# Token tiles taken out of step at the stage changes of a two-block transformer kernel

## The chip, the cores and the metric

The kernel runs on one core of one Trainium2 chip. The metric is the device time of one execution in microseconds. Time before the change: 2136.25 us, the median of 3 runs (2133.06 to 2136.64).

## What is computed

256 tokens of width 1024 in fp32. The first block (a mixer of three attention kinds, then a mixture of experts gathered row by row) is untouched by the change except for its very end. The second block is:

```
for layer in (0, 1):
    x = x + 0.5 * norm(swiglu(norm(x)))        # ffn0, ffn2
    h = norm(x)
    m = short_conv(h)      if layer == 0       # conv_in, conv_out
      = diff_attention(h)  if layer == 1       # q, k, v -> o
    x = x + norm(m)
    x = x + 0.5 * norm(swiglu(norm(x)))        # ffn1, ffn3
    if layer == 0: k, v = norm(x) @ w_kv       # shared keys and values
```

Each norm is an RMS norm over the 1024 columns with its own gain. swiglu has 2816 hidden columns.

## The kernel before

**Tiling.** The tokens are two tiles (t = 0, 1) of 128. Every weight matrix is read in blocks ("panels") of 1 MB, 1024 x 256 or 256 x 1024 words. The list of panels is written once (`plan_panels`, lines 65 to 101), with the PSUM bank of each, and all engines follow it by semaphores that count panels. SyncE loads panel p into `raw[p % 3]` as soon as panel p - 3 is split (`load`, L411). Products are kept exact by splitting each fp32 operand into a high part (ScalarE copy to fp32r, L669) and a low part (VectorE subtraction, L1106), and by three matmuls per product (`exact3`, L1767: high x high, high x low, low x high, all recorded at L1759). ScalarE and VectorE split panel p once panel p - 3 is used.

**Two forms of a block.** `panel_a` keeps 128 weight columns stationary and moves 256 tokens (output: features on partitions). `panel_b` keeps 128 tokens stationary and moves 256 weight columns (output: tokens on partitions). Both are 48 matmuls of 256 columns.

**An ffn** (`ffn`, L2082) has 11 steps of a gate, an up and a down block. Gate goes to bank 0, up to bank 1; ScalarE takes silu (L960), VectorE the product (L1585), both split it into `ah`, `al` (L965, L1590). Down blocks add into four accumulator banks `ACC[2t + half]` over all steps: 24 matmuls of 512 columns, first tile 0 then tile 1. Steps 2 to 10 are a loop; the last down block stands alone.

**A stage change** (`post`: ScalarE L988, VectorE L1611, POOL L625). When tile t's sums are complete, ScalarE squares the 1024 columns (L995), POOL makes rstd (L529, L532), VectorE multiplies by the gain (L1619) and adds to x (L1622). Then the next norm: ScalarE squares and scales tile 0 (L1002, L1004), VectorE tile 1 (L1110, L1630). TensorE waits for both tiles and transposes 16 squares of 128 x 128 into `ACC` (`turn`, L1816); ScalarE and VectorE write them, 256 wide, times the gain of the next norm as `xh` (L708) and `xl` (L1127). The first block of the next stage starts on k = 0 as soon as its low part is there. ScalarE and VectorE split the next stage's first two panels before `post`.

**Around it.** conv_in is 12 blocks in the order b, c, u for each quarter; conv_out and o are `project` (L2112), four blocks of token-stationary matmuls straight into `ACC`, the last one's tile 0 announced by `branch_half`. After ffn1 the rows are normed for kv (8 blocks: 4 of k, 4 of v), and the same transposes, still in `ACC`, are written again with another gain for ffn2 (`turn("f2")`, L1037). q (4 blocks) comes after ffn2. In `turn("diff")` the normed attention output is transposed, and `project("o")` waits for all eight low parts (L2200).

```
2101  panel_a(p0, stream=f"f{f}")       # first gate block, waits for xl piece by piece
2102  panel_a(p0 + 1)
...
2137  for t in range(TT):
2138      pe.wait_ge(rows_ready[t], XIDX["f0"] + 1)
2139  turn("f0", xn)
```

Of the kernel before, what the change touches and what calls it, by code (L numbers as in the profile page):

```python
# [26 lines left out]
P = 128  # L27
# [37 lines left out]
def plan_panels():  # L65
# [3 lines left out]
    def add(name, count, pieces=1, words=PANEL, banks=(0, 1)):  # L69
        for j in range(count):  # L70
            b = banks[j % len(banks)] if banks else None
            plan.append((name, pieces, words, b))
# [20 lines left out]
    add("conv_in", 12, banks=(0, 1, 2))  # L93
    add("conv_out", 4, banks=())
    ffn("ffn1")
    add("kv", 8)
    ffn("ffn2")
    add("q", 4)
# [15 lines left out]
EVAC = [sum(b is not None for b in BANK[:p]) for p in range(NP + 1)]  # L114


XPOSE = [("mix", 4), ("hg", 2), ("peer", 4), ("f0", 4), ("conv", 4), ("f1", 4), ("kv", 4), ("attn", 4), ("diff", 4), ("f3", 4)]
XBASE = {n: sum(b for _, b in XPOSE[:k]) for k, (n, _) in enumerate(XPOSE)}
XEND = {n: XBASE[n] + b for n, b in XPOSE}
XIDX = {n: k for k, (n, _) in enumerate(XPOSE)}  # L120

_splits = [(n, 2 * b) for n, b in XPOSE]
_splits.insert(XIDX["kv"] + 1, ("f2", KD))
SBASE = {n: sum(b for _, b in _splits[:k]) for k, (n, _) in enumerate(_splits)}
SEND = {n: SBASE[n] + b for n, b in _splits}
# [18 lines left out]
SUMS = {n: sum(m not in HEAD_NORMS for m, *_ in NORMS[:k + 1]) for k, (n, *_) in enumerate(NORMS)}  # L144
# [3 lines left out]
X_AT = {n: 2 * (k + 1) for k, n in enumerate(["peer", "final", "p0", "pc", "p1", "p2", "pa", "p3"])}  # L148

POSTS = [("p0", "conv"), ("pc", "f1"), ("p1", "kv"), ("p2", "attn"), ("pa", "f3"), ("p3", None)]  # L150
# [10 lines left out]
def build(nc, io):  # L161
    ctx = ExitStack()
    with ctx:
# [6 lines left out]
        def over(name, shape, at, skip=0):  # L170

            return nc.alloc_sbuf_tensor_at(name, shape, F32, offset=place[at] + skip)
# [124 lines left out]
        top[0] = 0  # L297
        ff_s, ff_a = carve(2, T), carve(2, T)
        causal = carve(len(BLOCKS), P)
        cv_b, cv_c, cv_z = carve(2, T), carve(2, T), carve(2, T)  # L300
        cv_u = carve(2, T + CONV_W - 1)
        df_k, df_v, df_q = carve(DIFF_HEADS, T), carve(TT, D), carve(DIFF_HEADS, T)
# [3 lines left out]
        df_o = carve(TT, D)  # L306
        df_mx, df_sum, df_r = carve(4, TT), carve(4, TT), carve(4, TT)
        sq_dump = carve(D)
        lam_in, lam_dot, lam_exp, lam = carve(4, HD), carve(2), carve(2), carve(1)
# [7 lines left out]
        def bank(b):  # L317
            return PS[:, b, :] if b < 4 else ACC[:, b - 4, :]

# [14 lines left out]

        sumsq = [sem(f"sumsq{t}") for t in range(TT)]
# [4 lines left out]
        branch_half = sem("branch_half")  # L340
# [67 lines left out]
        def _(sp):  # L408
# [50 lines left out]
            def load_ffn(f):  # L459
# [11 lines left out]
                if f == 0:  # L471
                    sp.wait_ge(v_used, UNITS * PE_K)
                load(p0 + 1, column(up, 0))
                with sp.Fori(1, FF_STEPS) as i:
                    load(p0 + 2, column(gate, i), 3, i - 1)
                    load(p0 + 3, column(up, i), 3, i - 1)
                    load(p0 + 4, down_rows(i - 1), 3, i - 1)
                load(p0 + 3 * FF_STEPS - 1, down_rows(FF_STEPS - 1))

            load_ffn(0)  # L480
            p0 = FIRST["conv_in"]
            for j in range(4):
                for w in range(3):
                    load(p0 + 3 * j + w, rows_1024(io["w_conv_in_2"][0], w * D + j * PC))
            for j in range(4):
                load(FIRST["conv_out"] + j, rows_1024(io["w_conv_out_2"][0], j * PC))
            load_ffn(1)
            for j in range(8):
                load(FIRST["kv"] + j, rows_1024(io["w_kv_2"], j * PC))
            load_ffn(2)  # L490
# [1730 lines left out]
```

## Time and profile before

| | |
|---|---|
| median of 3 runs | 2136.25 us |
| profiled execution, its own time | 2136.16 us |
| its span, first to last instruction | 2134.3 us |
| TensorE busy | 1898.1 us, 89% |
| VectorE, ScalarE, POOL busy | 60%, 36%, 20% |
| mean granted TensorE clock | 0.938 of 2.4 GHz |
| HBM read | 494.53 MB, 232 GB/s over the span |

The span runs from the first to the last instruction of the profiled execution; the rest of its own time lies around it. From 0 to about 430 us is the first block's mixer, to 1062 us the experts, then ffn0, conv (from 1273), ffn1 (from 1379), kv (from 1577), ffn2 (from 1626), q and attention (from 1825), o (from 1903), ffn3 (from 1939 to 2126).

### The profile page before, as it was taken

What the parts mean: (1) busy time and instruction counts of PE and PEld (TensorE: products, weight loads), DVE (VectorE), ACT (ScalarE), POOL (GpSimd) and SP (SyncE); (2) the same over time, 40 slices, a digit from 0 to 9 for tenths busy, and PEclk for the clock granted to TensorE, in tenths of its full rate; (3) what the DMA queues carried; (4) which work ended last, traced back from release to release, by engine and by line L of the source; (5) the groups of instructions that cost most, each with busy time, mean ns of one, the idle gap of its engine ahead of it and who ended that gap; (6) DMA issues with size and microseconds to landing.
All of it is one profiled execution on the core that took longest, in us unless ns stands there. A gap on an engine that the chain in (4) does not pass through costs nothing.

```text
span 2134.3 us, 30642 instructions
## 1 busy us (share of the span) xinstructions
PE 1898.1 (89%) x11270; PEld 1530.4 (72%) x11270; DVE 1286.3 (60%) x2439; ACT 764.9 (36%) x1183; POOL 423.0 (20%) x536
## 2 busy tenths in 40 slices
PE   7999999777788778887799989899989999768998
PEld 7999999733333333333389989899989999668997
DVE  4546955787777777775554556654454445655444
ACT  4346233321221221221144344433444344544433
POOL 4000000276545545455200010000010000110000
PEclk9989999889989989889999999999999999869999
DMA  8324265499999999999765545465545555314552
GB/s 229 100 81 116 60 187 161 156 421 422 421 422 422 421 422 421 422 421 422 311 206 186 187 150 175 152 194 179 193 149 178 178 191 181 99 49 151 191 181 99
DMA packets 231409, 496.65 MB, mean 233 GB/s; under 512 B 21653, under 2 KB 182566, under 8 KB 198566
## 3 DMA queue, kind: packets, MB, share of 16 engines
q1 hardware_dynamic: 188432, 221.36, 33.1%
q0 software_dynamic: 38224, 273.04, 31.0%
q10 hardware_dynamic: 4678, 1.21, 0.3%
q8 instruction: 52, 0.85, 0.2%
q14 instruction: 23, 0.19, 0.0%
HBM read 494.53 MB, written 1.05 MB: 232 GB/s over the span
## 4 chain that ended last, share of the span: by engine, by line
PE 67%; DMA 15%; DVE 7%; issue 4%; POOL 4%; ACT 3%; another core or an unknown queue 0%; DVEq 0%; POOLq 0%; ACTq 0%
PE ps L1759 43%; PE acc L1759 22%; DMA rows_hi<-in_peer_uv,idx_now 13%; POOL raw L614 1%; DMA rows_xh<-in_peer_uv,idx_now 1%; PE acc L1816 1%; POOL rstd L532 1%; POOL arena L614 1%; DVE lo L1106 1%; DVE arena L1486 0%; DVE arena L1482 0%; DVE arena L1489 0%; ACT hi L669 0%; ACT xh L708 0%
## 5 line engine op out<-in xcount | busy, mean ns | idle before, releaser
L1106 DVE TENSOR_TENSOR lo<-raw,hi 128x2048 fp32r<-128x2048 f32 x210 | 479.5, 2284 | 382.3 <-ACT hi L669 382.2
L1759 PE MATMUL ps<-xh,hi 128*128 128x256 f32 x2184 | 626.1, 287 | 7.1 <-DVE xl L1127 5.9
L1759 PE MATMUL ps<-xl,hi 128*128 128x256 f32 x2184 | 622.7, 285 | 0.0
L1759 PE MATMUL ps<-xh,lo 128*128 128x256 f32 x2184 | 622.3, 285 | 0.0
L669 ACT ACTIVATE hi<-raw 128x2048 fp32r<-128x2048 f32 x210 | 400.1, 1906 | 336.7 <-PE ps L1759 276.4
L1759 PEld LDWEIGHTS ps<-xh,hi 128*128 128x128 f32 x2184 | 423.7, 194 | 13.4 <-issue 10.3
L1759 PEld LDWEIGHTS ps<-xl,hi 128*128 128x128 f32 x2184 | 423.7, 194 | 1.5
L1759 PEld LDWEIGHTS ps<-xh,lo 128*128 128x128 f32 x2184 | 423.3, 194 | 0.1
L529 POOL TENSOR_SCALAR ss<-ss 128x1 f32<-128x1 f32 (+2 forms) x34 | 11.6, 342 | 1181.5 <-ACT arena L995 942.0
L1759 PE MATMUL acc<-arena,diag 128*128 128x512 f32 x384 | 189.0, 641 | 48.0 <-ACT diag L941 47.9
L1759 PE MATMUL acc<-rows,diag 128*128 128x512 f32 x192 | 120.7, 794 | 79.5 <-ACT diag L941 63.2
L1759 PEld LDWEIGHTS acc<-arena,diag 128*128 128x128 f32 x384 | 74.4, 200 | 152.7 <-issue 81.6
L1759 PEld LDWEIGHTS acc<-rows,diag 128*128 128x128 f32 x192 | 48.0, 259 | 151.7 <-issue 133.5
L1511 DVE SCALAR_TENSOR_TENSOR arena<-arena,xn 128x1024 f32<-128x1024 f32 x96 | 115.3, 1223 | 44.6 <-DMA arena<-in_peer_uv,idx_now 44.6
L941 ACT ACTIVATE diag<-ident,arena 128x128 f32<-128x128 f32 x256 | 81.8, 390 | 160.8 <-DVE arena L1520 153.4
L937 ACT ACTIVATE arena<-arena 128x4 f32<-128x4 f32 x64 | 13.3, 208 | 331.8 <-DVE arena L1511 161.5
L1759 PE MATMUL acc<-hi,ah 128*128 128x512 f32 x320 | 125.0, 391 | 0.0
L1759 PE MATMUL acc<-lo,ah 128*128 128x512 f32 x320 | 125.0, 391 | 0.0
L1759 PE MATMUL acc<-hi,al 128*128 128x512 f32 x320 | 124.5, 389 | 0.0
L614 POOL DMA_INDIRECT arena<-in_peer_uv,idx_now x96 | 115.4, 1202 | 26.3 <-issue 24.4
L674 ACT ACTIVATE arena<-ps 128x512 f32<-128x512 f32 (+1 forms) x54 | 32.0, 592 | 143.4 <-PE ps L1759 143.4
L1511 DVE SCALAR_TENSOR_TENSOR rows<-rows,xn 128x1024 f32<-128x1024 f32 x48 | 58.6, 1225 | 34.8 <-DMA rows<-in_peer_uv,idx_now 34.8
(279 smaller groups left out, 2853.4 us busy)
## 6 DMA issues: line engine op xcount, KB each, us to landing
raw<-in_w_ffn_gate SPq DMA_DIRECT2D x44, 1024.0 KB, 5.3
raw<-in_w_ffn_up SPq DMA_DIRECT2D x44, 1024.0 KB, 5.3
raw<-in_w_ffn_down SPq DMA_DIRECT2D x44, 1024.0 KB, 5.0
raw<-in_w_in SPq DMA_DIRECT2D x29, 1024.0 KB, 5.5
raw<-in_w_conv_in SPq DMA_DIRECT2D x12, 1024.0 KB, 5.2
raw<-in_w_kv SPq DMA_DIRECT2D x8, 1024.0 KB, 5.4
raw<-in_w_out SPq DMA_DIRECT2D x4, 1024.0 KB, 5.0
raw<-in_peer_w_q SPq DMA_DIRECT2D x4, 1024.0 KB, 5.2
```

What stands on the lines that cost most here:

```text
L529: g.tensor_scalar(m, m, scale / factor ** 2, EPS / factor ** 2, ALU.mult, ALU.add).then_inc(rstd_step, 1)
L532: g.tensor_tensor(rs, m, minus_half[:, c], ALU.pow).then_inc(rstd_ready[t], 1)
L614: g.indirect_dma_start(out=rows[k], out_offset=None, in_=io["peer_uv"], in_offset=bass.IndirectOffsetOnAxis(ap=idx_now[:, k:k + 1], axis=0))\
L669: nc.scalar.activation(hi[s][:, 0:WORDS[p]], raw[s][:, 0:WORDS[p]], ACT.Copy).then_inc(hi_done, 1)
L674: nc.scalar.activation(out, bank(BANK[p]) if in_ is None else in_, func, scale=scale).then_inc(evacuated, 1)
L937: nc.scalar.activation(pe_gelu[:, own], pe_h[:, own], ACT.Gelu).then_inc(gelu_done, 1)
L941: nc.scalar.activation(diag[:, k % DIAGS, :], ident[:, :], ACT.Copy, scale=pe_act[:, k:k + 1]).then_inc(diag_ready, 1)
L1106: v.tensor_tensor(lo[s][:, 0:WORDS[p]], raw[s][:, 0:WORDS[p]], hi[s][:, 0:WORDS[p]].bitcast(F32), ALU.subtract).then_inc(lo_done, 1)
L1511: v.scalar_tensor_tensor(out=rows[k][:, 0:D], in0=rows[k][:, 0:D], scalar=1.0, in1=xn[:, t, :], op0=ALU.mult, op1=ALU.mult, accum_out=pe_h ...
L1759: return nc.tensor.matmul(out, l, r, start=first, stop=last)
L1816: last = nc.tensor.transpose(ACC[:, b, j * T + t * P:j * T + (t + 1) * P], rows[:, t, c:c + P], ident[:, :])
```

## The change

1. **Spare block.** A fourth place (`spare_raw`, `spare_hi`, `spare_lo`) is carved from the arena, and seven panels go through it: the first up block of each ffn, a block of conv_in (c, quarter 0), of kv (v, quarter 1), and of k (quarter 1). SyncE loads it and both engines split it near the end of the stage before. To make room, `df_k`, `df_v` move over `oh`, `ol`, and `df_o` over `xn`.
2. **Last two down blocks of an ffn, and last two blocks of `project`,** are taken tile by tile: tile 0 of both, then tile 1 of both. The ffn loop is one step shorter, and `sum_ready` announces half rows.
3. **`post`** works on half rows of 512 columns, the two engines sharing each tile: square, product, update, square of x, scale. Tile 0 goes through to its normed rows before tile 1's product. POOL's order is post 0, next 0, post 1, next 1, and the factor 1/D is taken into the squares.
4. **Transposes per tile** (`turn_tile`): 8 squares in groups of 2, 3, 3 into banks that differ by tile, then 128-wide copies to `xh`, `xl` on both engines.
5. **The next stage's first two blocks are token-stationary** (`first_pair`): tile 0 of the first block, tile 0 of the spare, then tile 1's transposes, tile 1 of both. (ffn0: both tiles of the first block, then the spare.) What an ffn or conv_in needs with features on partitions is transposed back: 4 squares in an ffn, 8 in conv.
6. **The second panel of a stage** is split after `post`, no longer before it.
7. **kv** has its own copy `kvh`, `kvl`, so `xh`, `xl` for ffn2 are written while kv runs. kv computes v and half of k; k's quarters 0 and 1 move behind ffn2, one before tile 0's transposes for q and one before tile 1's.
8. **`turn("diff")`** uses the PS banks, and `project("o")` waits for the low parts one by one.

The diff, cut to its core:

```diff
@@ plan @@
     def ffn(name):
-        for i in range(FF_STEPS):
+        add(name, 1, spare=1)
+        for _ in range(1, FF_STEPS):
             add(name, 2)
-            if i:
-                add(name, 1, banks=())
+            add(name, 1, banks=())
         add(name, 1, banks=())
...
-    add("kv", 8)
+    add("kv", 1, spare=1)
+    add("kv", 4)
     ffn("ffn2")
+    add("q", 1, spare=1)
     add("q", 4)
@@ SyncE @@
+            def load_spare(s, src):
+                if s:
+                    sp.wait_ge(spare_lo_done, s)
+                else:
+                    sp.wait_ge(v_used, UNITS * PE_K)
+                sp.dma_start(spare_raw.rearrange("p (k n) -> p k n", k=KD), src).then_inc(spare_ready, 16)
...
                 with sp.Fori(1, FF_STEPS) as i:
-                    load(p0 + 2, column(gate, i), 3, i - 1)
+                    load(p0 + 1, column(gate, i), 3, i - 1)
...
+                if following is not None:
+                    load_spare(s + 1, following)
+                load(p0 + 3 * FF_STEPS - 2, down_rows(FF_STEPS - 1))
@@ POOL @@
             def post(name):
                 load_gain(name)
-                norm(name)
+                after = dict(POSTS)[name]
+                for t in range(TT):
+                    norm_tile(name, t)
+                    if after:
+                        norm_tile(after, t)
@@ ScalarE @@
+            def turn_tile(name, t, out=xh):
+                for g, ks in enumerate(TILE_KS):
+                    if name in TURN_AT:
+                        act.wait_ge(tile_turned[t], TURN_AT[name] + g + 1)
+                    else:
+                        act.wait_ge(tile_lo[t], TILE_AT[name] - KD + ks[-1] + 1)
+                    for k in ks:
+                        c = GAIN[name] + k
+                        nc.scalar.activation(out[:, k, t * P:(t + 1) * P], turned_tile(t, k), ACT.Copy, scale=cols[:, c:c + 1]).then_inc(tile_hi[t], 1)
...
                 i = FF_STEPS - 1
+                split(p0 + 3, 3, i - 1)
                 split(p0 + 4, 3, i - 1)
-                split(p0 + 5, 3, i - 1)
-                silu(p0 + 2, 3, i - 1)
-                upper(p0 + 2, p0, 3, i - 1, fh)
-                for p in range(last + 1, min(last + 3, NP)):
-                    split(p)
+                if following is not None:
+                    split_spare(following)
+                silu(p0 + 1, 3, i - 1)
+                upper(p0 + 1, p0, 3, i - 1, fh)
+                if last + 1 < NP:
+                    split(last + 1)
...
+                square(0, 0)
+                square(0, 1)
...
+                square_x(0)
+                square(1, 0)
+                scale_x(0)
+                square(1, 1)
+                if between is None:
+                    turn_tile(after, 0, out)
+                square_x(1)
+                scale_x(1)
+                if between is not None:
+                    split(between)
+                    turn_tile(after, 0, out)
@@ VectorE @@
+                product(0)
+                update(0)
+                if after is not None:
+                    square_x(0)
+                    scale_x(0)
+                product(1)
+                if after is not None and between is None:
+                    turn_tile(after, 0, out_hi, out_lo)
+                update(1)
...
+                square_x(1)
+                scale_x(1)
+                if between is not None:
+                    split(between)
+                    turn_tile(after, 0, out_hi, out_lo)
+                turn_tile(after, 1, out_hi, out_lo)
@@ TensorE @@
+            def first_pair(stage, stream, lh=xh, ll=xl):
+                p, s = FIRST[stage], SPARE[stage]
+                def tile(w, t):
+                    return token_tile(None if w else p, t, bank(w)[:, t * PC:(t + 1) * PC], lh=lh, ll=ll, stream=stream)
+                for t in range(TT):
+                    if stream in TURN_AT:
+                        turn_tile(stream, t)
+                    if not t:
+                        begin(p)
+                    last = tile(0, t)
+                    if t:
+                        last.then_inc(panel_used, 1)
+                    if stage != "ffn0":
+                        if not t:
+                            begin_spare(p, s)
+                        last = tile(1, t)
...
+                first_pair(f"ffn{f}", stream)
                 panel_a(p0 + 1)
+                pe.wait_ge(evacuated, EVAC[p0] + 2)
+                rows = ff_a.rearrange("p f t -> p (f t)")
+                for j in range(2):
+                    for t in range(TT):
+                        last = nc.tensor.transpose(bank(3)[:, j * T + t * P:j * T + (t + 1) * P],
+                                                   rows[:, t * PC + j * P:t * PC + (j + 1) * P], ident[:, :])
+                last.then_inc(ff_turned, 1)
                 panel_a(p0 + 2)
...
+                p = p0 + 3 * FF_STEPS - 5
+                panel_a(p)
+                panel_a(p + 1)
+                begin(p + 2)
+                pe.wait_ge(ff_lo, FF_STEPS * (f + 1) - 1)
+                for half in range(2):
+                    down_part(p + 2, 0, half)
+                begin(p + 3)
+                pe.wait_ge(ff_lo, FF_STEPS * (f + 1))
+                for half in range(2):
+                    down_part(p + 3, 0, half, u=(fh, fl), final=True).then_inc(sum_ready, 1)
+                for half in range(2):
+                    last = down_part(p + 2, 1, half)
+                last.then_inc(panel_used, 1)
+                down_part(p + 3, 1, 0, u=(fh, fl), final=True).then_inc(sum_ready, 1)
+                down_part(p + 3, 1, 1, u=(fh, fl), final=True).then_inc(panel_used, 1)
...
+            panel_a(p0, rh=kvh, rl=kvl)
+            turn_tile("attn", 0)
+            begin_spare(p0, SPARE["q"])
+            for f in range(2):
+                last = feature_tile(None, f, bank(1)[:, f * T:(f + 1) * T], rh=kvh, rl=kvl)
+            last.then_inc(spare_used, 1)
+            turn_tile("attn", 1)
             for j in range(4):
-                panel_a(FIRST["q"] + j, stream=None if j else "attn")
+                panel_a(p0 + 1 + j, stream=None if j else "attn")
```

## Rows read from the trace of the kernel before

**Rows 1.** The page: busy time of each engine, share, instructions.
```profile
PE 1898.1 (89%) x11270; PEld 1530.4 (72%) x11270; DVE 1286.3 (60%) x2439; ACT 764.9 (36%) x1183; POOL 423.0 (20%) x536
```

**Rows 2.** Waits of TensorE from 1075 us: engine, line, releaser, us, times, longest.
```profile
PE acc L1816 <- ACT xn L1004: 31.4, 5, 6.8
```

**Rows 3.** Stretches at the changes: us, busy and count per engine, PEclk, DMA share, GB/s.
```profile
1262.10:1272.93 10.83, 3.76 (x17) 3.30 (x17) 6.47 (x9) 4.91 (x10) 5.17 (x7) 0.74 0.46 148
1369.80:1379.19 9.39, 3.66 (x17) 3.30 (x17) 6.18 (x8) 4.91 (x10) 3.98 (x7) 0.68 0.44 161
1566.50:1577.27 10.77, 3.71 (x17) 3.31 (x17) 6.42 (x9) 4.92 (x10) 5.16 (x7) 0.72 0.46 148
1623.90:1625.93 2.03, 0.01 (x1) 0.03 (x1) 0.63 (x2) 1.99 (x6) 0.00 (x0) 0.97 0.73 220
1814.20:1825.09 10.89, 3.83 (x17) 3.31 (x17) 6.53 (x9) 4.91 (x10) 4.25 (x6) 0.63 0.30 98
1929.20:1938.58 9.38, 3.65 (x17) 3.31 (x17) 6.17 (x8) 4.92 (x10) 3.99 (x7) 0.70 0.45 158
```

**Rows 4.** The chain that ended last: start, us, what.
```profile
1074.42 24.07 PE ps L1759 x192
...
1103.96 11.51 PE ps L1759 x96
1115.47 5.47 PE acc L1759 x24
...
1379.19 23.65 PE ps L1759 x192
...
1625.93 24.72 PE ps L1759 x192
...
1825.09 24.20 PE ps L1759 x192
```

**Rows 5.** Timeline of the change into conv: start, us, engine, line, operation, idle before.
```profile
1251.15 0.40 PE L1759 MATMUL acc<-hi,ah 128*128 128x512 f32 x1
...
1262.25 1.02 ACT L995 ACTIVATE arena<-acc 128x1024 f32<-128x1024 f32 x1 [1.60 <-PE acc L1759]
...
1263.73 0.56 POOL L532 TENSOR_TENSOR rstd<-ss,minus_half 128x1 f32<-128x1 f32 x1
...
1264.75 1.28 DVE L1622 SCALAR_TENSOR_TENSOR x<-xn,rstd,x 128x1024 f32<-128x1024 f32 x1
...
1264.85 1.24 POOL L529 TENSOR_SCALAR ss<-ss 128x1 f32<-128x1 f32 x1 [0.56 <-ACT arena L1002]
...
1266.17 1.54 POOL L532 TENSOR_TENSOR rstd<-ss,minus_half 128x1 f32<-128x1 f32 x1
...
1267.73 1.15 ACT L1004 ACTIVATE xn<-x,rstd 128x1024 f32<-128x1024 f32 x1 [2.98 <-POOL rstd L532]
...
1271.43 3.03 ACT L708 ACTIVATE xh<-acc,cols 128x256 fp32r<-128x256 f32 x8 [2.55 <-PE acc L1816]
...
1272.30 3.23 DVE L1127 SCALAR_TENSOR_TENSOR xl<-acc,cols,xh 128x256 fp32r<-128x256 f32 x8 [2.90 <-ACT xh L708]
...
1272.93 0.55 PE L1759 MATMUL ps<-xh,hi 128*128 128x256 f32 x1 [0.26 <-DVE xl L1127]
```

**Rows 6.** The page: the two halves of a block's split.
```profile
L1106 DVE TENSOR_TENSOR lo<-raw,hi 128x2048 fp32r<-128x2048 f32 x210 | 479.5, 2284 | 382.3 <-ACT hi L669 382.2
...
L669 ACT ACTIVATE hi<-raw 128x2048 fp32r<-128x2048 f32 x210 | 400.1, 1906 | 336.7 <-PE ps L1759 276.4
```

**Rows 7.** Timeline of ScalarE: four diagonal copies of 128x128.
```profile
1044.55 1.28 ACT L941 ACTIVATE diag<-ident,arena 128x128 f32<-128x128 f32 x4 [0.23 <-DVE arena L1520]
```

**Rows 8.** Timeline of VectorE before ffn0: second tile's rows.
```profile
1069.07 1.35 DVE L1571 TENSOR_SCALAR xn<-x,rstd 128x1024 f32<-128x1024 f32 x1 [0.95 <-POOL rstd L532]
```

**Rows 9.** Timeline of TensorE at the o projection's first matmul.
```profile
1903.39 0.58 PE L1759 MATMUL acc<-hi,xh 128*128 128x256 f32 x1 [2.91 <-DVE xl L1127]
```

**Rows 10.** Waits of TensorE over the whole span.
```profile
PE acc L1759 <- issue: 16.4, 3, 6.7
```

More of the change, by code:

```diff
@@ L657, in _ @@
             post("pa")
-            norm("f3")
             post("p3")
@@ L1005, in post @@
-                turn(after, xh, after)
-            split(FIRST["ffn0"] + 1)
-            turn("f0", xh, "f0")
-            ffn(0)
-            post("p0", FIRST["conv_in"])
-            p0 = FIRST["conv_in"]
-            def conv(j):
-                for w, out in enumerate((cv_b, cv_c, None)):
-                    split(p0 + w + 2, 3, j)
-                    if out is not None:
-                        wait(act, cv_y, j)
-                        evac(p0 + w, out.rearrange("p f t -> p (f t)"), m=3, i=j)
+                square_x(0)
@@ L1037, in _ @@
-            act.wait_ge(panel_used, FIRST["ffn2"])
-            turn("f2", xh, "f2")
-            ffn(2)
-            post("p2", FIRST["q"])
-            for j in range(4):
-                p = FIRST["q"] + j
-                split(p + 2)
-                evac(p, df_q[:, 2 * j:2 * j + 2, :].rearrange("p h t -> p (h t)"), scale=HD ** -0.5)
+            conv_high(0)
+            with act.Fori(1, 4) as j:
+                for w, out in enumerate((cv_b, cv_c, None)):
+                    split(p0 + 1 + w, 3, j)
+                    if out is not None:
+                        act.wait_ge(cv_y, j)
+                        evac(p0 + 2 + w, out.rearrange("p f t -> p (f t)"), m=3, i=j - 1)
+                conv_high(j)
@@ new lines, in _, with evac_v @@
+            split_spare(SPARE["ffn1"])
+            for j in range(3):
+                split(FIRST["conv_out"] + j + 2)
+            post("pc", project_sums("pc", "conv_out"))
+            turn_tile("f1", 1)
+            ffn(1, SPARE["kv"])
+            post("p1", down_sums("p1", 1), out=kvh)
+            turn_tile("kv", 1, kvh)
+            p0 = FIRST["kv"]
+            def evac_v(j, b):
+                nc.scalar.activation(df_v[:, :, j * PC:(j + 1) * PC], bank(b).rearrange("p (t n) -> p t n", t=TT), ACT.Copy).then_inc(evacuated, 1)
@@ L1748, in _ @@
             turn("diff", xh, xl, "diff")
-            for j in range(4):
+            for j in range(3):
                 split(FIRST["o"] + j + 2)
@@ new lines, in ffn, with down_part, down @@
+            def ffn(f, stream):
+                p0 = FIRST[f"ffn{f}"]
+                def down_part(p, t, half, u=(ah, al), first=False, final=False):
+                    wh, wl = views(p, 2)
+                    for k in range(2):
+                        c, w = slice(t * P, (t + 1) * P), slice(half * 512, (half + 1) * 512)
+                        last = exact3(ACC[:, 2 * t + half, :], u[0][:, k, c], u[1][:, k, c], wh[:, k, w], wl[:, k, w],
+                                      first and k == 0, final and k == 1)
+                    return last
+                def down(p, i, m=0, r=0, first=False):
```

552 lines of the change are left out of this document (358 added, 194 removed).

## The prediction

> **What bounds the kernel now.** I read the page first: TensorE is busy 89% of the span and no other engine over 60% [rows 1]. That alone does not say where time can be had, so I asked for TensorE's waits in the second half, from 1075 us on, which is what the change touches. The five stage changes stand out: 31.4 us in five waits for a tile's normed rows, the largest group by far [rows 2]. The table of stretches shows each change from the last matmul of one stage to the first of the next: 10.83, 9.39, 10.77, 10.89 and 9.38 us, with some 17 TensorE instructions (the transposes) in each and a granted clock of 0.63 to 0.74 [rows 3], so the engine spends part of it, and the transposes, at 1.2 GHz. A sixth, shorter one (2.03 us) stands before the third FFN. Between the changes TensorE is back to back: 96 matmuls in 11.51 us, a block of 48 is 5.76 us, a down block of 24 is 5.47 us [rows 4]. The chain through one change is in the timeline of the first [rows 5]: square, product, update, square, rstd, scale, transposes, high copy, low copy, and it starts only when all sums of the tile are complete.
>
> A full-clock start is late too: from 1379.19 us four blocks take 23.65 us instead of 23.02 (0.6 lost), after the 2.03 us gap they take 24.72 (1.7 lost), and from 1074.42 24.07 (1.05 lost) [rows 4].
>
> **The parts, on a clock S = start of the second last down block, 1251.15 us [rows 5].** Half of 24 matmuls is 2.73 us.
>
> *Last two down blocks by tile.* Matmuls are the same, in another order: tile 0 of both (5.47), then tile 1 of both (to S+10.9). Tile 0's sums are complete at S+5.5 plus a drain, instead of S+8.2. The spare block's split (1.91 us on ScalarE, 2.28 on VectorE, [rows 6]) now stands ahead of silu and product: I estimate that the last low part of the activation comes at S+3.05 where S+2.7 is wanted, 0.35 us of TensorE wait. Taken once in each ffn with a following stage.
>
> *Tile 0's chain.* Whole-row operations of 1.02 (square), 1.28 (update) and 1.15 us (scale) [rows 5] become two halves, some 0.6 to 0.7 each, shared between the engines. Square to S+6.7; rstd on POOL 0.2 + 0.56 with its hops 0.95, S+7.85 (product beside it); update S+9.2; square S+9.95; rstd S+10.9; scale S+11.6. The two POOL operations of 1.24 and 1.54 us [rows 5] overlap VectorE's update and square; in the new order VectorE waits for them, so I take the 0.56 kind. The last matmul ends at S+11.2, so the rows are ready 0.3 to 0.5 us after it: the 6.8 us wait goes. What is late next is the split of the turned tile. ScalarE still has the last square (to S+12.2), then eight copies of 128x128 instead of 256 wide. 256 wide, eight take 3.03 us on ScalarE and 3.23 on VectorE [rows 5], a spacing of 0.36 and 0.39. The price of 128 wide is bounded below by half of that and above by no gain at all. The nearest row is the diagonal copy, four of 128x128 in 1.28 us, 0.3 each [rows 7]; I take 0.29 and 0.27. Cutting the pieces in half so saves a fifth to a third of each and costs a third to a half more in all. With these values TensorE's first matmul comes at S+13.6, tile 0 of the first block ends at S+16.1, tile 0 of the spare block at S+19.0.
>
> *Tile 1's chain* runs under these: update S+16.9, square S+17.6, rstd S+18.55, scale S+19.25, transposes, split, first matmul S+20.75; tile 1 of the first block ends S+23.4 (paced by the split), of the second S+26.3. The next block's split, now queued behind the turned tile on both engines, is done at S+26.1: just in time, and if it is late, TensorE waits for it. Before: 1272.93 [rows 5] is S+21.8, plus 0.6 and 11.52, S+33.9.
>
> **Terms.** (1) into conv: 33.9 - 26.3 = 7.6, less eight more transposes (0.9, at full clock) = 6.6. (2) into kv: the same without transposes, 7.5; its 10.77 us row agrees with the first. (3) conv_out into ffn1: only the first three steps before the end differ. Here a tile of two blocks, 5.76 us, covers the chain wholly; first block pair ends at E+14.8 after the last matmul E. Before E + 9.39 + 0.6 + 11.52 = E+21.5. 6.7 less four transposes (0.45) = 6.2. (4) o into ffn3 the same, 6.3. (5) into attn: the first key block (5.76) needs nothing and covers tile 0's chain; then transposes, the second key block to E+12.45, transposes, a split of about 1.6 us in view, two feature tiles: E+19.65 for three blocks. Before E + 10.89 + 1.15 (24.20 less 23.02, taken from this start's row [rows 4]) + 17.28 = E+29.3. 9.65, less 0.35 for the wait in the ffn and 0.3 for the next split = 9.0. (6) into ffn2: the gap of 2.03 us and the slow start of 1.7 [rows 3, 4] go, since the other normed copy is made during kv; less four transposes, 3.2. This costs ScalarE and VectorE 16 small pieces (4.6 and 4.3 us) over the kv blocks, where ScalarE, at 1.91 for a split and 0.6 for a copy out, has 3.2 us spare per block and VectorE 3.5: nothing, under the cover of two blocks; without it, their 4.6 us. (7) diff into o: the first matmul no longer waits for all eight low copies; eight take 3.23 us [rows 5], the first is out 2.7 us before the last, and the wait that ended with the last was 2.91 us [rows 9]: 2.6. (8) into ffn0: tile 0 is turned in VectorE's waits; tile 1's rows come at 1070.4 as before [rows 8], and the spare block is split after both tiles, low part ready at about 1079.2, TensorE done at 1085.0 instead of 1086.97 (1074.42 + 24.07 - 11.52): 2.0 less 0.45 = 1.5. Between -1 (the spare lands late, since it is loaded only when the last row is used) and 3. (9) The end: the last square is half as long, 0.5.
>
> Sum 6.6 + 7.5 + 6.2 + 6.3 + 9.0 + 3.2 + 2.6 + 1.5 + 0.5 = 43.4. I take 0.5 us off for each of five changes for hops I did not count, 2.5: 40.9. At nothing go: seven spare loads in place of seven ordinary ones (same bytes; SP issues each behind a wait that is long satisfied, except into ffn0), the moved key blocks (same matmuls), the key, value and output buffers' new places, more small semaphore steps on POOL, which is idle nearly throughout. Their cover is the slack of ScalarE and VectorE per block; without it a block would start up to 2.3 us late, once a stage.
>
> The sum stands against the profiled execution, 2136.16 us (span 2134.3 and 1.86 around it), 0.1 under the median of 2136.25: 2095.3 us.
>
> **The clock** is the largest unknown. After the idle gap of 2.03 us the grant fell at its end and 1.7 us were lost [rows 3, 4]. My new gaps are 0.4 and 1.2 us before tile 0, with transposes between, and 1.75 us with transposes in it before tile 1. Whether the transposes hold the clock up decides. In the rows, the changes with transposes lost only 0.6 us at the matmuls that followed, the gap without any 1.7: they count for something, so I take no fall.
>
> **Rivals.** *(a) The clock falls at both handoffs.* Price 1.7 us twice at four changes and once at attn, 15.3 at most, some hidden behind tile 1's chain: about 13, so 2108 us. For it: 1.75 is near 2.03. Against: the rows just named, the 0.6 us after transposes against 1.7 without. Chance 17%. The Trainium skill, "TensorE: Matmul & The Clock Gate", Part 4, states that a transpose does not count as busy in the same way; by that rule this rival is the outcome. The trace agrees only in that the transposes themselves ran slow. *(b) The next splits come late.* ScalarE and VectorE serve in order, and the next block's split is behind the turned tile with 0.2 us margin. If small pieces cost as much as the 256-wide ones, each change loses about 2 x 0.8 + 2, some 18 us in five: 2113. Chance 9%. *(c) Better than summed*, since tile 1 is paced by less or update and square overlap further: 1.2 us more at each, 2089 or a little less. Chance 10%. *(d) Slower:* the straight-line code of TensorE grows (last two ffn steps and the pairs are written out). The waits of the whole span have "issue" ones of up to 6.7 us, three in all [rows 10], in which nothing seen holds the engine. If every one of seven stage changes got one at a code edge, 46.7 us come back: 2142. It decides from 5.8 us at each. Against it: the present loop ends show none. 2%. *(e) It does not do what it says:* the last down block's activation comes late, so that tile 0 is not early; then each ffn's change gains only the spare blocks and the halved operations, 3 of 4 changes keep half: some 28 us left, 2122. 4%.
>
> **Numbers.** The sum's own case has 58% (2091 to 2102 us). About 0.2% (4.3 us) is what a measurement of this kernel can tell from none. The range takes in (a), most of (c) and the low bounds of small pieces: 2086 to 2112. Faster 0.96, same 0.02, slower 0.02.
>
> **What would show it.** TensorE's 31.4 us of waits for rows gone, replaced by waits of about 1 us for low copies; tile 0's rows scaled within 0.5 us of the last sum; the stretch from a stage's last matmul to the next stage's first real matmul under 3 us, at clock 1.0; ffn steps of 16.98 us unchanged. Wrong would be: granted clock 0.5 in these stretches, waits on splits L669 or L1106 over 1 us, issue waits, or a first pair that ends later than S+28.

## The result and the profile after

The changed kernel takes 2097.13 us, the median of 4 runs (2095.51 to 2100.67), against 2136.26 us: ratio 0.9823, 95% interval 0.9809 to 0.9838. Run again (e5), beside its own runs of before (2132.78 us), it took 2098.23 us, ratio 0.9836 (0.9823 to 0.9850). The forecast of 2095.3 is a ratio of 0.9808, at the edge of the first interval and 2.8 thousandths under the second ratio: right in size, and some 2 to 6 us too hopeful. One execution further down, the profiled one of e8 (2309 us at a mean granted clock of 0.75), fell in a slower state that the chip shows at times: it is left out of e8's figures, and its trace is not read.

The page of the kernel after: its head and its first row (busy us, share, instructions).

```profile
span 2093.7 us, 30883 instructions
...
PE 1883.2 (90%) x11294; PEld 1515.1 (72%) x11294; DVE 1297.5 (62%) x2534; ACT 777.5 (37%) x1280; POOL 410.2 (20%) x536
```

TensorE executes more instructions than before and is busy 15 us less: of the 40.6 us that the span lost, 15 are matmuls and transposes that ran faster (partly by chance, see conv_out and o below), the rest is waiting. TensorE's waits from 1060 us on (us in total, times, longest):

```profile
PE ps L2498 <- DVE arena L1954: 10.7, 7, 4.1
PE ps L1990 <- DVE xl L1727: 8.5, 9, 2.5
...
PE acc L1990 <- DVE ol L1884: 2.2, 1, 2.2
PE ps L1990 <- DVE spare_lo L1733: 2.1, 1, 2.1
...
PE acc L1990 <- DVE ol L1773: 0.5, 3, 0.2
PE ps L2331 <- DVE xn L1833: 0.4, 2, 0.2
```

The first row is a wait inside attention, which the kernel before has too (10.5 us). The 31.4 us of waits for a tile's normed rows [rows 2] are 0.4 us now. What is late in their place is the split of the turned tile (L1727), 8.5 us in nine waits (4.1 of them at ffn0's start), and the last activation of the ffn (L1773), 0.2 us three times. The stretches from a stage's last matmul to the next stage's first real one, in columns as in [rows 3]: into conv, ffn1, kv and ffn3, and fifth a stretch of ffn0's start.

```profile
1261.71:1263.82 2.11, 1.09 (x9) 0.89 (x9) 1.87 (x5) 2.11 (x8) 0.86 (x2) 1.00 0.00 0
1361.00:1362.99 1.99, 1.12 (x11) 0.89 (x9) 1.67 (x4) 1.99 (x8) 0.86 (x2) 1.00 0.00 0
1552.50:1554.56 2.06, 1.09 (x9) 0.89 (x9) 1.82 (x5) 2.06 (x8) 0.86 (x2) 1.00 0.00 0
1894.80:1896.76 1.96, 1.11 (x10) 0.90 (x9) 1.66 (x4) 1.96 (x8) 0.86 (x2) 1.00 0.00 0
...
1068.00:1074.00 6.00, 5.96 (x26) 5.59 (x26) 2.88 (x7) 0.91 (x4) 4.97 (x11) 0.50 1.09 366
```

At these four changes, stretches of 9.38 to 10.83 us at a granted clock of 0.68 to 0.74 [rows 3] became 1.96 to 2.11 us at 1.00. Only ffn0's start runs at 1.2 GHz. The change into conv in the timeline, as in [rows 5]:

```profile
1261.94 0.44 PE L2331 MATMUL ps<-ident,xn 128*128 128x128 f32 x2 [0.24 <-DVE xn L1833]
...
1263.09 1.66 ACT L1029 ACTIVATE xh<-acc,cols 128x128 fp32r<-128x128 f32 x6
...
1263.82 0.36 PE L1990 MATMUL ps<-hi,xh 128*128 128x256 f32 x1 [0.79 <-DVE xl L1727]
1264.01 1.64 DVE L1727 SCALAR_TENSOR_TENSOR xl<-acc,cols,xh 128x128 fp32r<-128x128 f32 x6
```

The second last down block starts at S = 1250.18 us here, so the first real matmul is at S+13.6, as summed. The stage ends are read from the chain (start, us, what), against [rows 4]:

```profile
1097.52 5.47 PE acc L1990 x24
...
1342.16 18.98 PE acc L1990 x156
...
1388.32 5.47 PE acc L1990 x24
...
1614.07 5.47 PE acc L1990 x24
...
1791.99 23.34 PE ps L1990 x192
...
1858.67 2.57 PE ps L1990 x12
...
1870.33 24.59 PE acc L1990 x192
...
1922.08 5.47 PE acc L1990 x24
```

| stretch, up to | before | after | gained in it | summed |
|---|---|---|---|---|
| last expert matmul | 1062.04 | 1061.65 | 0.4 | none |
| ffn0's first down block | 1098.49 | 1097.52 | 0.6 | 1.5 |
| conv_out's first matmul | 1349.37 | 1342.16 | 6.2 | 6.6 |
| ffn1's first down block | 1402.84 | 1388.32 | 1.5 + 5.8 | 6.2 |
| ffn2's first down block, less two moved key blocks | 1650.66 | 1614.07 | 10.5 | 10.7 |
| end of q, with them | 1849.29 | 1815.33 | 8.9 | 9.0 |
| end of attention | 1889.08 | 1858.67 | -3.5 | 0 |
| o's first matmul | 1903.39 | 1870.33 | 2.65 | 2.6 |
| ffn3's first down block | 1962.40 | 1922.08 | 1.2 + 6.0 | 6.3 |
| end | | | 0.3 | 0.5 |

The 1.5 and 1.2 us are conv_out's and o's own matmuls, which ran faster (18.98 us for 156, where before's took 20.46 us; 24.59 against 25.82 us [rows 4]). The column of gains sums to 40.6. It compares one execution with one: ffn0's 0.6 is no firmer than conv_out's 1.5 (see e7).

### The profile page after: what moved, and what is told of

It is laid out like the page before. It is cut to its first block, busy times and chain, and to the rows that moved or that the text cites. A ratio compares the mean times of both kernels' runs of the same rounds, so it can differ in the third digit from the quotient of the medians.

```text
span 2093.7 us, 30883 instructions
## 1 busy us (share of the span) xinstructions
PE 1883.2 (90%) x11294; PEld 1515.1 (72%) x11294; DVE 1297.5 (62%) x2534; ACT 777.5 (37%) x1280; POOL 410.2 (20%) x536
## 3 DMA queue, kind: packets, MB, share of 16 engines
HBM read 494.53 MB, written 1.05 MB: 237 GB/s over the span
## 4 chain that ended last, share of the span: by engine, by line
PE 66%; DMA 16%; DVE 8%; POOL 4%; issue 4%; ACT 2%; DVEq 0%; POOLq 0%; ACTq 0%
PE ps L1990 43%; PE acc L1990 22%; DMA rows_hi<-in_peer_uv,idx_now 14%; DMA rows_xh<-in_peer_uv,idx_now 2%; POOL raw L682 1%; POOL arena L682 1%; DVE arena L1648 1%; DVE arena L1644 1%; DVE arena L1651 1%; POOL rstd L600 0%; POOL idx_now L677 0%; DVE lo L1268 0%; DVE arena L1939 0%; DVE arena L1591 0%; ACT diag L1008 0%
## 5 line engine op out<-in xcount | busy, mean ns | idle before, releaser
L1268 DVE TENSOR_TENSOR lo<-raw,hi 128x2048 fp32r<-128x2048 f32 x203 | 463.2, 2284 | 315.0 <-ACT hi L737 314.9
L1990 PE MATMUL ps<-xh,hi 128*128 128x256 f32 x1960 | 559.7, 286 | 4.1 <-DVE xl L1289 2.3
L1990 PE MATMUL ps<-xl,hi 128*128 128x256 f32 x1960 | 556.9, 284 | 0.0
L1990 PE MATMUL ps<-xh,lo 128*128 128x256 f32 x1960 | 556.9, 284 | 0.0
L737 ACT ACTIVATE hi<-raw 128x2048 fp32r<-128x2048 f32 x203 | 386.1, 1905 | 270.3 <-PE ps L1990 243.2
L1990 PEld LDWEIGHTS ps<-xh,hi 128*128 128x128 f32 x1960 | 377.8, 193 | 8.0 <-issue 5.0
L1990 PEld LDWEIGHTS ps<-xl,hi 128*128 128x128 f32 x1960 | 377.9, 193 | 1.5
L1990 PEld LDWEIGHTS ps<-xh,lo 128*128 128x128 f32 x1960 | 377.6, 193 | 0.1
L595 POOL TENSOR_SCALAR ss<-ss 128x1 f32<-128x1 f32 x22 | 6.6, 299 | 906.8 <-ACT arena L1086 876.3
L1990 PE MATMUL ps<-hi,xh 128*128 128x256 f32 (+1 forms) x272 | 80.2, 295 | 11.6 <-DVE xl L1727 8.0
```

The lines of the kernel that those rows point to most:

```text
L595: g.tensor_scalar(m, m, ss[:, k, TT + t:TT + t + 1], BIAS[name], ALU.add, ALU.add).then_inc(rstd_step, 1)
L737: nc.scalar.activation(hi[s][:, 0:WORDS[p]], raw[s][:, 0:WORDS[p]], ACT.Copy).then_inc(hi_done, 1)
L1268: v.tensor_tensor(lo[s][:, 0:WORDS[p]], raw[s][:, 0:WORDS[p]], hi[s][:, 0:WORDS[p]].bitcast(F32), ALU.subtract).then_inc(lo_done, 1)
L1990: return nc.tensor.matmul(out, l, r, start=first, stop=last)
```

## The experiments

All kernels are the changed one with one edit, if not said otherwise. Stages are compared by the same first matmuls as in the table, since the experts upstream of it end up to 3 us apart from one execution to the next. Only the tile order, the spare block's place, two splits and the wait before o were changed alone. The halved operations of `post`, kv's own copy and the moved key blocks were not: what each of them gives is in the sum of the table, but not shown apart.

### Order alone, filler alone, neither

```diff
@@ e1: the last two down blocks, and project's, block by block again @@
-                for half in range(2):
-                    down_part(p + 2, 0, half)
+                for t in range(TT):
+                    for half in range(2):
+                        last = down_part(p + 2, t, half)
+                last.then_inc(panel_used, 1)
                 begin(p + 3)
...
-                for half in range(2):
-                    last = down_part(p + 2, 1, half)
-                last.then_inc(panel_used, 1)
...
                 tile(2, 0)
+                tile(2, 1).then_inc(panel_used, 1)
                 begin(p + 3)
                 tile(3, 0).then_inc(sum_ready, 1)
-                tile(2, 1).then_inc(panel_used, 1)
@@ e2: the spare block behind both tiles of the first one, in every stage @@
-                    if stage != "ffn0":
-                        if not t:
-                            begin_spare(p, s)
-                        last = tile(1, t)
-                if stage == "ffn0":
-                    begin_spare(p, s)
-                    for t in range(TT):
-                        last = tile(1, t)
+                begin_spare(p, s)
+                for t in range(TT):
+                    last = tile(1, t)
@@ e3: both @@
```

> The changed kernel, with only the order of the last two down blocks and of the last two blocks of conv_out and o put back (both tiles of the one, then both of the other). Theory (tile 0's early sums carry its chain under the last matmuls): tile 0's sums come 2.7 us later in an ffn and 2.9 us later in a projection, its rows are ready some 3 us after the last matmul, and the first matmul of conv, ffn1, kv and ffn3 comes about 1.8 us later each, not later in q, where a key block lies over it: 7 us slower than the changed kernel, and up to 6 more if TensorE's clock falls in the longer gap. Rival (the spare block and the halved operations do it all): 0 to 1 us.

> The changed kernel, with the spare block's two tiles both after the first block's two tiles at every stage, as it is at ffn0. Theory (the spare block's tile 0 covers tile 1's chain): TensorE ends tile 0 of the first block about 4.4 us before tile 1's first matmul can start instead of 1.5 us before: 2.8 us more at each of conv, ffn1, kv and ffn3, 11 us slower, and more if the clock falls in a gap of over 3 us (up to 1.7 each). Rival (the early sums do it all): 0 to 1 us.

> Both of the first two edits together. If early sums and spare block each cover another wait, their prices add: 18 us slower than the changed kernel, 22 to 26 with the clock's fall. If one stands in for the other, it costs much more than the two prices' sum, near all of the four changes' gain of 26 us.

Measured: e1 2115.12 us (ratio 0.9908, 0.9892 to 0.9925), e2 2111.61 (0.9890, 0.9874 to 0.9907), e3 2119.04 (0.9934, 0.9916 to 0.9953). Against the changed kernel's 2097.13 us that is 18, 14 and 22 us more. e1 costs more than forecast (7, up to 13 with the clock), e2 what was forecast with the clock (11 to 18). Both together cost 22, inside the forecast of 22 to 26 for prices that add, and yet less than the 32 of the two measured prices. The timeline of e1 at the change into conv, TensorE only:

```profile
1263.65 0.69 PE L2331 MATMUL ps<-ident,xn 128*128 128x128 f32 x2 [2.95 <-DVE xn L1833]
1264.13 1.49 PE L2331 MATMUL acc<-ident,xn 128*128 128x128 f32 x6
```

and of e2 (the wait before tile 1):

```profile
1272.71 0.44 PE L2331 MATMUL ps<-ident,xn 128*128 128x128 f32 x2 [2.41 <-DVE xn L1833]
```

Their chains, e1 first, then e2, then e3:

```profile
1265.62 7.84 PE ps L1990 x48
...
1283.74 0.87 PE ps L2458 x8
```

```profile
1274.25 13.12 PE ps L1990 x96
1287.37 0.87 PE ps L2454 x8
```

```profile
1271.26 11.83 PE ps L1990 x96
1283.09 0.87 PE ps L2453 x8
```

In e1 TensorE is idle for 2.95 us before tile 0's rows; then the transposes take twice their time (1.49 us for six, 0.82 in the changed kernel), and the first 48 matmuls take 7.84 us where the changed kernel needs 6.00. In e2 the idle time is 2.41 us before tile 1, the transposes still run at full clock here, and the grant falls behind them: 96 matmuls in 13.12 us, 11.83 in e3. The stretch from S (1250.18, 1249.80, 1253.57, 1248.26) to the eight transposes back, which are the same work in all, is 29.9 us in the changed kernel, 33.9 in e1, 33.8 in e2 and 34.8 in e3.

So e1 on top of e2 costs 1.0 us at this change, where alone it costs 4.0. The rows say which part does not add. VectorE starts to write tile 1's normed rows (L1833) at S+18.6 in the changed kernel and in e2, and at S+20.9 in e1 and in e3: without the order they come 2.3 us later, with filler or without, and that price is paid both times. The clock is what is not paid twice. In e3 the slow matmuls of tile 0 are over before tile 1's rows are there, and the pause before tile 1 is 0.83 us where it was 2.41, so that tile 1's 96 matmuls run at full clock again:

```profile
1269.72 0.44 PE L2331 MATMUL ps<-ident,xn 128*128 128x128 f32 x2 [0.83 <-DVE xn L1833]
```

By stages (into conv with ffn1; kv; attention; ffn3) e1 lost 8.3, 4.8, 2.6 and 4.0 us, e2 7.5, 3.5, -0.1 and 4.4, e3 12.0 (1.5 of it the chance at conv_out told below), 5.1, 1.2 and 5.6.

### What of e1 is clock, and do transposes hold it up?

The pause of e1 is filled with work that nobody reads: 20 transposes in e9, 20 matmuls in e10.

```diff
@@ on top of e1, in turn_tile @@
+                if not t and name in ("conv", "f1", "kv", "f3"):
+                    for _ in range(20):
+                        nc.tensor.transpose(bank(2)[:, 0:P], ident[:, :], ident[:, :])
                 pe.wait_ge(rows_ready[t], ROWS_AT[name] + 1)
@@ e10 instead @@
+                        mm(bank(2)[:, 0:T], ah[:, 0, 0:P], ah[:, 0, :], True, True)
```

> The kernel without tile order (e1) with 20 transposes of the identity, 128x128, put on TensorE in the pause of 2.95 us before tile 0's rows are there, at the changes into conv, ffn1, kv and ffn3; they fill 2.7 us and nobody reads them. Theory A, transposes hold the granted clock up: the stage's own transposes and first block then run at 2.4 GHz (48 matmuls in about 6.0 us instead of 7.84, 7.28, 8.47 and 7.49; the transposes 0.7 us shorter), so about 9 us faster than e1 in all, near 2106 us, and what is left to the changed kernel (9 to 10 us) is the 2.73 us of order at each change. Theory B (the Trainium skill, TensorE: Matmul & The Clock Gate, Part 4, a transpose does not count as busy): the clock falls as in e1, granted clock 0.5 in the first block, 2115 us, no difference over 1 us.

> The same as e9 with 20 real matmuls (128x256, one pass) in place of the 20 transposes, in the same pause, 2.4 us. Both theories: the clock holds, first blocks of about 6.0 us, near 2106 us. If it still falls, the clock is not set by the pause, and e9 tells nothing.

Measured: e9 2111.11 us (0.9896, 0.9881 to 0.9911), e10 2112.55 (0.9907, 0.9892 to 0.9922). Timeline and chain of e9 at the change into conv:

```profile
1263.60 2.34 PE L2326 MATMUL ps<-ident 128*128 128x128 f32 x20
1266.71 0.44 PE L2334 MATMUL ps<-ident,xn 128*128 128x128 f32 x2 [0.77 <-DVE xn L1833]
...
1268.59 5.99 PE ps L1990 x48
```

Its windows over the 20 transposes, the stage's own transposes and the first block (granted clock third from the right):

```profile
1263.60:1265.90 2.30, 2.30 (x21) 2.10 (x19) 1.44 (x4) 1.30 (x4) 0.64 (x2) 1.00 0.05 18
1266.70:1268.50 1.80, 1.09 (x8) 0.85 (x8) 1.56 (x4) 1.80 (x8) 0.86 (x2) 1.00 0.00 0
1268.60:1274.40 5.80, 5.80 (x48) 5.80 (x49) 4.26 (x12) 2.38 (x7) 1.50 (x3) 1.00 0.00 0
```

and e10's first block at the same place:

```profile
1267.90 5.99 PE ps L1990 x48
```

The four first blocks of e9 take 5.99, 5.98, 5.94 and 6.00 us, where e1's took 7.84, 7.28, 8.47 and 7.49: these transposes hold TensorE at 2.4 GHz just as matmuls do (e10: 5.99, 6.00, 5.94, 5.98). That is theory A. Chance is no likely rival: e3 has e1's pauses too, and the clock fell after all eight of them (2.77 to 2.95 us), while it held at all eight places that e9 and e10 fill. By stages e9 is 1.7, 2.5 and 1.5 us shorter than e1 (into conv with ffn1, kv, ffn3), 5.7 in all and not 9; conv_out's matmuls happened to lose 1.5 us in e9 and none in e1 (see below), so the clock's part at these four changes is 7.2 us.

At q, where e9 fills nothing, e1 and e9 both lose 2.6 us against the changed kernel. The pause before the q blocks is 2.11 and 2.17 us in them, and in e3 and e10 it is 2.17 and 2.16, but the matmuls behind it differ (e1, then e3):

```profile
1805.74 24.77 PE ps L1990 x192
```

```profile
1808.19 23.27 PE ps L1990 x192
```

In e9 they take 24.78 us, and in e10, where the stage loses 1.2 us, 23.27. So 1.5 of the 2.6 us is clock as well, 8.7 us of e1's 19.7 in all. The rest, 11.1 us, is the order itself: 2.3 into conv, 2.8 into ffn1, 2.3 into kv, 1.2 at q and 2.5 into ffn3. The medians of e1 and e9, each against its own runs of before, differ by less than their intervals; the clock is shown by the rows.

### Attention

```diff
@@ e4: split of o's second block, ScalarE and VectorE @@
-            split(p0 + 6)
             act.wait_ge(lam_dots, 2)
...
-            for j in range(3):
+            for j in range(-1, 3):
                 split(FIRST["o"] + j + 2)
@@ e6: the same, and ffn3's spare block as well @@
-                if j == 2:
-                    split_spare(SPARE["ffn3"])
...
+            split(FIRST["o"] + 1)
+            split_spare(SPARE["ffn3"])
             for j in range(3):
                 split(FIRST["o"] + j + 2)
```

> The changed kernel, with the split of o's second block moved from before the attention to after it on ScalarE and VectorE. Theory (the attention starts late because the added spare block's split pushes this one past the last q block): the attention's first VectorE operation comes 2.2 to 3.7 us earlier and the kernel is as much faster than the changed one. Rival (the late start is the table load or POOL's copies of q and k): 0.

> The split of o's second block and the split of ffn3's spare block both moved behind the attention. Theory: VectorE has nothing left of splits after the last q block, the attention starts as soon after q as in the kernel before (2.5 us), 3.6 us faster than the changed kernel; the splits lie under the o blocks, where each engine has over 3 us per block. Rival: they delay o's third block, and 1 to 2 us are given back.

Measured: e4 2093.62 us (0.9811, 0.9794 to 0.9827), e6 2094.57 (0.9821, 0.9808 to 0.9835). The timeline behind the last q block, first of before (attention's first VectorE operation), then of the changed kernel, then of e4:

```profile
1851.84 0.56 DVE L1708 TENSOR_TENSOR arena<-acc,arena 128x384 f32<-128x384 f32 x1
```

```profile
1815.84 1.90 ACT L737 ACTIVATE hi<-raw 128x2048 fp32r<-128x2048 f32 x1
...
1817.76 1.28 ACT L1207 ACT_TABLE_LOAD   x1
1817.78 2.29 DVE L1268 TENSOR_TENSOR lo<-raw,hi 128x2048 fp32r<-128x2048 f32 x1 [1.26 <-ACT hi L737]
...
1818.34 1.99 POOL L720 COPY arena<-arena 128x256 f32 x1 [0.55 <-PE acc L1990]
...
1821.59 0.56 DVE L1939 TENSOR_TENSOR arena<-acc,arena 128x384 f32<-128x384 f32 x1
```

```profile
1818.14 0.56 DVE L1937 TENSOR_TENSOR arena<-acc,arena 128x384 f32<-128x384 f32 x1 [0.23 <-PE acc L1988]
```

Attention's first VectorE operation comes 2.55 us after q's last matmul in before, 6.26 us in the changed kernel, 2.9 in e4 and 2.55 in e6. Before, VectorE's part of the split of o's second block was done at 1848.3 us, ahead of q's end at 1849.3. The added split of ffn3's spare block in the q loop pushes it past q's end (L737, L1268 in the second fence), in front of attention on both engines. With it gone, the stretch from ffn2's first down block to o's first matmul is 253.2 us (e4) and 252.4 (e6), against 256.3: e4 gives back 3.1 of the 3.5 us, e6 all of it. The table load and POOL's copies are still there, so the rival of e4 is out; o's blocks take 25.17 us in e6 but 24.40 in e12, which has the same edit, so that of e6 is not borne out. The medians of e4 and e6 differ from the changed kernel's by less than the intervals; the gain is shown by the rows. One POOL copy of 256 columns took 1.99 us beside VectorE's subtraction of two SBUF operands, and 0.40 us undisturbed.

### ffn0's start

```diff
@@ e7: ScalarE and VectorE @@
-            for t in range(TT):
-                turn_tile("f0", t)
-            split_spare(SPARE["ffn0"])
+            turn_tile("f0", 0)
+            split_spare(SPARE["ffn0"])
+            turn_tile("f0", 1)
```

> The changed kernel, with ffn0's spare block split between tile 0's and tile 1's turned pieces on both engines, not after both. Theory (the spare's split is what ends ffn0's first pair): TensorE's wait of 2.1 us for the spare's low part goes, 2.1 us faster than the changed kernel. Rival (the load lands too late for it and now holds up tile 1's pieces): 0 or up to 2 us slower.

Measured: 2095.10 us (0.9819, 0.9806 to 0.9832). The changed kernel here (VectorE, TensorE), then e7:

```profile
1067.64 0.86 DVE L1727 SCALAR_TENSOR_TENSOR xl<-acc,cols,xh 128x128 fp32r<-128x128 f32 x3
1068.04 0.58 PE L1990 MATMUL ps<-hi,xh 128*128 128x256 f32 x1 [2.46 <-DVE xl L1727]
...
1075.23 1.95 ACT L1035 ACTIVATE spare_hi<-arena 128x2048 fp32r<-128x2048 f32 x1
```

```profile
1068.44 1.91 ACT L1035 ACTIVATE spare_hi<-arena 128x2048 fp32r<-128x2048 f32 x1 [3.04 <-DMA arena<-in_w_ffn_up]
...
1071.98 2.27 DVE L1733 TENSOR_TENSOR spare_lo<-arena,spare_hi 128x2048 fp32r<-128x2048 f32 x1
```

From the last expert matmul to ffn0's first down block: 36.45 us before, 35.87 in the changed kernel, 33.35 in e7. In the changed kernel TensorE waits 2.46 us for tile 0's third to fifth squares, which VectorE takes only after tile 1's update and square; the grant falls, tile 1's transposes start at 1072.41 us though their rows are there by 1070.0, and the spare block is split behind all of it (2.1 us of wait). e7 takes the last of these away.

How much that is worth varies. In the ten traces that start ffn0 as the changed kernel does (its own, e1 to e6, e9 to e11) the stretch takes 35.0 to 37.3 us: in e2, e9, e10 and e11 the clock falls after the wait of 2.1 us, and these four are the ones of 37.0 and more. e7 with 33.35 and e12 with 34.0 us are below all ten, by 1 to 4 us. The one trace of before has 36.45, so that the change's own gain here lies between -0.9 and 1.5 us.

### The wait before o, and the changed kernel again

```diff
@@ e11 @@
-            project("o", xh, xl, stream="diff")
+            pe.wait_ge(turned_lo, SEND["diff"])
+            project("o", xh, xl)
```

> The changed kernel, but the o projection waits for all low parts again, as before the change (part 8 undone in part). My term of the prediction: the first matmul of o comes 2.6 us later. The 1.23 us by which o's four blocks were shorter in the changed kernel (24.59 against 25.82 us) I take for clock: the pause was shorter. If so they take 25.8 us again here, and the run is 3.8 us slower than the changed kernel, 2101; if the shorter blocks came from elsewhere, 2.6 us, 2099.7.

> The changed kernel again, unedited, beside the following ones on the same chip: 2095 to 2101 us, 0.982 of the kernel before.

Measured: e11 2099.21 us (0.9843, 0.9828 to 0.9858); e5 2098.23. The wait of before [rows 9] is back in e11, 2.9 us, and o's first matmul is 2.65 us later counted from ffn2 (258.91 against 256.26), as summed. The four o blocks take 24.94 us, not 25.8:

```profile
1873.72 24.94 PE acc L1990 x192
```

In the other runs with the short wait they take 24.29 to 25.17 us, so the pause is not what made them shorter than before's 25.82; with one execution of before that stays open. The changed kernel's second execution has this row at conv_out:

```profile
1341.48 0.58 PE L1990 MATMUL acc<-hi,oh 128*128 128x256 f32 x1 [2.19 <-DVE ol L1884]
...
1341.48 20.44 PE acc L1990 x156
```

The same kernel, the same pause (2.18 and 2.19 us), and the 156 matmuls take 20.44 us here and 18.98 in the first. The pause is 2.18 or 2.19 us in all thirteen traces. The 156 matmuls take 20.3 to 20.5 us in before, e4, e5 and e7, and 19.0 in the changed kernel's first execution, e2, e6, e11 and e12; where the order of the blocks is the old one, the 132 of the same piece of the chain take 17.6 us in e3, e9 and e10, and 16.1 in e1. Seven lose 1.4 to 1.5 us, six nothing. The 1.5 us that the table shows at conv_out are this, and no gain of the change.

### All three edits

e8 and e12 are one kernel, e6 with e7's edit.

> The two edits before together: 5.5 to 5.8 us faster than the changed kernel, about 2091.5 us.

> e8 again (both splits moved behind attention, ffn0's spare split between the two tiles' turned pieces), for an undisturbed profile. Against the changed kernel: the attention part gives back 3.5 us, ffn0 0 to 2 us; 2090 to 2093 us, faster than the kernel before by 1.9 to 2.1%.

Measured: e8 2090.39 us (median of five; 0.9799, 0.9785 to 0.9812), e12 2090.26 (0.9805, 0.9792 to 0.9819). In e12 ffn0's start takes 34.0 us, from ffn2's first down block to o 252.8, and the stages between are as in the changed kernel (290.80 us from ffn0's to ffn1's first down block in both). The edits bring 7 to 8 us over the changed kernel's medians, 5.9 in span, and this version is the fastest one measured.

## Why the prediction was right, and where not

**The chain and the handoffs: right.** First real matmul S+13.64 (S+13.6 summed), tile 1's first S+20.95 (20.75), the end of the pair near S+26.8 (26.3). The ffn's activation wait holds TensorE up by 0.33 us (0.35). Tile 0's rows come 0.24 us after the last matmul, a little sooner than given (0.3 to 0.5). Four times out of four the stretch is under 3 us at clock 1.0. Ffn steps are unchanged at 16.98 us.

**The price of small pieces: right in direction, a little high.** Six of 128x128 take 1.66 us on ScalarE and 1.64 on VectorE, a spacing of 0.26 where 0.29 and 0.27 were taken.

**The terms** into conv, ffn1, kv with ffn2, attention, o and ffn3 came out at 6.2, 5.8, 10.5, 8.9, 2.65 and 6.0, against 6.6, 6.2, 10.7, 9.0, 2.6 and 6.3. Five are a little short, 1.4 us in all; the 2.5 us taken off for uncounted hops was the right kind of reserve, and here it also paid for ffn0. (Redone from its own figures, terms 1, 2 and 6 are 0.1 us larger each; nothing hangs on it.)

**Rival (a), the clock: did not happen, and the reason given holds, though its evidence did not carry it.** The forecast said of transposes "they count for something, so I take no fall". It rested on one row with 0.6 us lost behind transposes; its own rows for q (24.20 us) and ffn0 (24.07) lose 1.2 and 1.05, nearer to the 1.7 of the gap without any. What shows it is e9, run afterwards. In the seven traces with the new order and spare block (the changed kernel, e4 to e7, e11, e12) no matmul at the 28 changes ran slow. Whether pauses this short (0.8 us) would have held the clock without transposes between them was not tested. The rule of the Trainium skill that stood beside this rival ("TensorE: Matmul & The Clock Gate", Part 4) would have e9's first blocks at 1.2 GHz; they ran at 2.4, so for these fp32 transposes the trace disagrees. The price of this rival was about right: in e1 the fall does happen, at 1.3 to 2.5 us a change.

**What failed first: "their cover is the slack of ScalarE and VectorE per block".** The forecast counted the spare block's split (1.91 and 2.28 us) as hidden by it, and named what it would cost without: a block "up to 2.3 us late, once a stage". It did not look at which work is queued behind it on ScalarE and VectorE. At q there is no slack left after the last block, because attention is run by these two engines; there the delay of the splits is a delay of the end, 3.5 us; e4 gives back 3.1 of it, e6 all.

**Second: term (8), ffn0.** Summed 1.5, measured 0.6 in this trace (-0.9 to 1.5 over the ten). The step that failed is "tile 0 is turned in VectorE's waits": only two of its eight squares are, the next three come after tile 1's update and square, and TensorE's pause of 2.46 us brings the grant down to 1.2 GHz until 1074 us. The split order costs another 1 to 4 us (e7).

**Where the sum was lucky.** 3.5 us lost in attention and 0.9 in ffn0 are offset in these two traces by 0.4 upstream, 1.5 at conv_out and 1.2 in o. The first two of these are shown to vary from one execution to another, and the third is open: o's blocks vary by 0.9 us among the later traces, but none takes the 25.82 us of before. Without the three, the traces give 37.5 us of gain, which lies between the two differences of medians, 39.1 and 34.6 us. The forecast of 40.9 should have been about 37.

**The theory on e1 to e3** was right on the mechanism and low on e1. The order was priced at 1.8 us at each of four changes and nothing at q, where a key block was said to lie over it; it costs 2.3 to 2.8 us at the four and 1.2 at q, and the clock 8.7 us where up to 6 were allowed. The e3 forecast met its number since order and filler do add; that the clock's falls do not, it did not say.

## What to carry to other kernels

When two tiles share the engines of a handoff, start one early and keep a block of work for the other's chain: to lose either half costs two thirds or more of what losing both costs (18 and 14 us against 22), because the idle time that is left also drops TensorE's clock. Cheap work on TensorE in a pause of 2.8 to 3 us (transposes did as well as matmuls) kept the grant up; it is for places where no real work can be had. Before a step is called hidden, list per engine what is queued behind it up to the next place where that engine, and not TensorE, sets the end. And compare two traces by stages, with a second execution of the same kernel beside them, before a microsecond is credited to the change.

## What the runs showed of the hardware

- These fp32 transposes of 128x128 hold the granted clock at 1.00 as matmuls do (e9, e10).
- The same pause in the same code gives either clock. After 1.65 or 1.66 us at ffn0's start TensorE was at 1.2 GHz within 0.5 us in three traces of nine (e1, e4, e5); after 2.11 to 2.17 us before q in two of four (e1, e9); after 2.18 or 2.19 us before conv_out in seven of thirteen.
- After 2.41 to 2.44 us (e2) and 2.77 to 2.95 us (e1, e3) it fell at all twelve changes. Pauses of 0.8 to 0.9 us at the handoffs, with transposes ahead of them, were not followed by it at any of the 28 in seven traces.
- Where it falls differs too: in e1 by the first transpose after the pause into conv (2.95 us), but only behind the eight transposes into ffn1 (2.77 us).
- A POOL copy of 128x256 takes 0.40 us, and one took 1.99 us while VectorE subtracted two SBUF operands (2.29 us).
